# The end of the sink attention: the gate's Silu in three pieces, the last values stored by VectorE, the first two gatings within the stage

## The reference

```python
def attention_mixer(h, norm_w, w_in, q_norm_w, k_norm_w, sinks, w_out):
    u = rms_norm(h, norm_w) @ w_in
    q, k, v, gate = jnp.split(u, [...], axis=-1)
    q = rms_norm(q.reshape(B, L, ATTN_HEADS, ATTN_HEAD_DIM), q_norm_w)
    k = rms_norm(k.reshape(B, L, ATTN_KV_HEADS, ATTN_HEAD_DIM), k_norm_w)
    ...
    o = banded_sink_attention(q, k, v, sinks)
    return (o * jax.nn.silu(gate)) @ w_out
```

## Time and profile before

| | us |
|---|---|
| Median of 3 runs | 1746.34 |
| Lowest, highest run | 1745.02, 1746.79 |
| Profiled execution, device time | 1750.94 |
| Its span in the trace | 1749.1 |
| TensorE busy in the span | 1671.2 |
| VectorE busy | 1188.2 |
| ScalarE busy | 896.5 |

### The profile page before, as it was taken

One profiled execution on the slowest core, in us unless ns is written; L12 is line 12 of the kernel. 1 busy time (PEld: TensorE's weight loads), 2 busy tenths in 40 slices (PEclk: granted clock), 3 DMA queues, 4 the chain that ended last, 5 costly groups with the idle time before them and its releaser, 6 DMA issues. The chain is left out here.

```text
span 1749.1 us, 34014 instructions
## 1 busy us (share of the span) xinstructions
PE 1671.2 (96%) x13060; PEld 1476.5 (84%) x13060; DVE 1188.2 (68%) x2002; ACT 896.5 (51%) x1562; POOL 72.3 (4%) x36
## 2 busy tenths in 40 slices
PE   7989989999999999989999999998989999899989
PEld 7887788899999999988888888896767898788877
DVE  5556566689989799976666666655746656556565
ACT  4335544454554677756666666633545553233333
POOL 0000000100000000000000000000002333100000
PEclk9979989999999999999999999999999999999899
DMA  6532144455555444445666666541123454200004
GB/s 217 181 101 93 49 146 156 158 184 164 180 168 175 137 127 128 133 127 188 193 192 192 192 194 194 174 151 37 61 72 97 145 148 146 81 3 2 3 26 144
DMA packets 63220, 230.06 MB, mean 132 GB/s; under 512 B 7024, under 2 KB 7280, under 8 KB 63104
## 3 DMA queue, kind: packets, MB, share of 16 engines
q1 hardware_dynamic: 63104, 228.44, 41.7%
HBM read 227.36 MB, written 1.05 MB: 131 GB/s over the span
## 5 line engine op out<-in xcount | busy, mean ns | idle before, releaser
L1077 DVE TENSOR_TENSOR tile_low<-weights,tile_high 128x1024 fp32r<-128x1024 f32 x252 | 307.1, 1221 | 143.1 <-ACT tile_high L1067 139.5
L1067 ACT ACTIVATE tile_high<-weights 128x1024 fp32r<-128x1024 f32 x252 | 268.2, 1064 | 136.6 <-issue 136.6
L178 ACT ACTIVATE tile_high<-weights 128x1024 fp32r<-128x1024 f32 x169 | 178.4, 1057 | 250.2 <-issue 76.7
L190 DVE TENSOR_TENSOR tile_low<-weights,tile_high 128x1024 fp32r<-128x1024 f32 x146 | 178.1, 1223 | 170.8 <-ACT tile_high L178 145.4
L1129 PE MATMUL banks<-parts,tile_high 128*128 128x256 f32 x2048 | 270.5, 285 | 0.3 <-PEq L999 0.3
L1431 PE MATMUL banks<-tile_high,parts 128*128 128x512 f32 x1024 | 254.6, 391 | 4.7 <-ACT parts L1396 4.7
L1129 PEld LDWEIGHTS banks<-parts,tile_high 128*128 128x128 f32 x2048 | 254.9, 192 | 0.9 <-issue 0.9
L1431 PEld LDWEIGHTS banks<-tile_high,parts 128*128 128x128 f32 x1024 | 193.2, 189 | 45.1 <-issue 4.9
L230 PE MATMUL banks<-parts,tile_high 128*128 128x272 f32 (+1 forms) x1216 | 171.8, 294 | 4.2 <-PEq L465 3.4
L230 PEld LDWEIGHTS banks<-parts,tile_high 128*128 128x128 f32 x1216 | 158.4, 192 | 19.4 <-issue 16.8
L1134 PE MATMUL banks<-parts,tile_low 128*128 128x256 f32 x1024 | 146.2, 286 | 9.2 <-DVE tile_low L1077 9.2
(11 more groups left out here) (383 smaller groups left out, 2265.7 us busy)
## 6 DMA issues: line engine op xcount, KB each, us to landing
weights<-in_peer_u SPq DMA_DIRECT2D x128, 512.0 KB, 3.5
weights<-in_peer_v SPq DMA_DIRECT2D x128, 512.0 KB, 3.5
weights<-in_dn_in SPq DMA_DIRECT2D x49, 512.0 KB, 3.5
weights<-in_in_t SPq DMA_DIRECT2D x19, 512.0 KB, 3.6
weights<-in_attn_t SPq DMA_DIRECT2D x19, 512.0 KB, 3.6
weights<-in_in_m SPq DMA_DIRECT2D x16, 512.0 KB, 3.6
weights<-in_wq SPq DMA_DIRECT2D x16, 512.0 KB, 3.5
weights<-in_dn_out SPq DMA_DIRECT2D x16, 512.0 KB, 3.5
```

Source lines behind the costliest of these rows:

```text
L178: k.nc.scalar.activation(k.high[:, m % 2, :], k.ring.view(n), ACT.Copy).then_inc(*k.high_made.up())
L190: unit.tensor_tensor(k.low[:, m % 2, :], k.ring.view(n), k.high[:, m % 2, :].bitcast(F32), ALU.subtract).then_inc(*k.low_made[engine].up())
L1067: k.nc.scalar.activation(k.high[:, (s + j) % 2, :], k.ring.buf[:, j % RING, :], ACT.Copy).then_inc(k.high_made.sem, 1)
L1077: k.nc.vector.tensor_tensor(k.low[:, (s + j) % 2, :], k.ring.buf[:, j % RING, :], k.high[:, (s + j) % 2, :].bitcast(F32), ALU.subtract).th ...
```

## The change

The Silu over the gate, one instruction over eight tiles, becomes three: over tiles 0 and 1 straight behind the last gate copy, and so ahead of the store of unit 14 and the copies of unit 15; over tiles 2 and 3, and over tiles 4 to 7, behind those copies. ScalarE's loop loses its last iteration. VectorE gets three instructions at the end of its list: the products of value chunks 0 and 1 with their gate, of chunks 2 and 3 with theirs, each after the Silu piece of the same number and after a count of stores, and the copy of unit 15's values out of PSUM, which ScalarE made before. `out_rows` is told by `opened=2` that two of the four gatings are done: it leaves them out on VectorE, ScalarE doesn't wait for them, and the counts of the other two move down by two.

```diff
@@ -1508,6 +1508,9 @@
     dve.wait_ge(*sig.last())
 
 
+OPENED = 2
+
+
 def sink_attention_stage(k):
 
 
@@ -1517,6 +1520,7 @@
     scaled, turned, unturned, summed = k.start("att_scaled", "att_turned", "att_copied", "att_valued")
     stored, stats, gated = k.start("att_stored", "att_stats", "gate_made")
     fills = AH // 2
+    silu, opened = k.start("gate_silu", "gate_opened")
     gate_tile = lambda i: k.tiles["attn_g"] + i
     ahead = dict(zip(range(2, 18, 2), [gate_tile(i) for i in range(AHEAD, fills)] + list(early(k, "attn_out"))))
     high, low = k.pair(L)
@@ -1634,6 +1638,15 @@
                     scale(u - 1)
                 if u in ahead:
                     make_low(dve, k, ahead[u])
+            for c in range(OPENED):
+                dve.wait_ge(*silu.at(c + 1))
+                dve.wait_ge(*stored.at(len(units) - 4 + 2 * c))
+                pair = k.y2[:, 2 * c:2 * c + 2, :]
+                nc.vector.tensor_tensor(pair, pair, T[:, GATE + 2 * c:GATE + 2 * c + 2, :], ALU.mult).then_inc(*opened.up())
+            tt, a = units[-1]
+            dve.wait_ge(*summed.at(len(units)))
+            nc.vector.tensor_copy(k.y2[:, a, META + tt * P:META + tt * P + P],
+                                  ps[:, value_bank(len(units) - 1), 0:P]).then_inc(*opened.up())
 
         @block.scalar
         def _(act):
@@ -1666,7 +1679,7 @@
                 nc.scalar.activation(k.y2[:, a, cols], ps[:, value_bank(u), 0:P], ACT.Copy).then_inc(*stored.up())
 
             stats2, = k.start("att_meta_copied")
-            for u in range(len(units) + 2):
+            for u in range(len(units) + 1):
                 if u < len(units):
                     exps(u)
                 if u in ahead:
@@ -1674,14 +1687,16 @@
                 if u and u % 2 == 0:
                     act.wait_ge(k.ring.used.sem, gate_tile(u // 2 - 1) + 1)
                     nc.scalar.activation(T[:, GATE + u // 2 - 1, :], fill, ACT.Copy).then_inc(*gated.up())
-                if u >= 2:
+                if u == len(units):
+                    act.wait_ge(*gated.at(fills))
+                    nc.scalar.activation(T[:, GATE:GATE + 2, :], T[:, GATE:GATE + 2, :], ACT.Silu).then_inc(*silu.up())
+                if 2 <= u <= len(units):
                     store(u - 2)
                 if 1 <= u <= len(units):
                     copy_turned(u - 1)
-                if u == len(units):
-                    act.wait_ge(*gated.at(fills))
-                    nc.scalar.activation(T[:, GATE:GATE + fills, :], T[:, GATE:GATE + fills, :],
-                                         ACT.Silu).then_inc(*gated.up())
+            for c, n in ((2, 2), (4, fills - 4)):
+                nc.scalar.activation(T[:, GATE + c:GATE + c + n, :], T[:, GATE + c:GATE + c + n, :],
+                                     ACT.Silu).then_inc(*silu.up())
 
 
 def heads_stage(k, xs, weights, spans):
@@ -1831,7 +1846,7 @@
     if stop <= 24: return
     out_rows(k, "attn_out", [(k.hm, 0, META, 0)] + [(k.h[:, tt, :], 2 + 2 * tt, P, META + tt * P) for tt in range(NT)],
              k.y2, k.tiles["dn_in"] + RING, k.T2[:, 10:18, :],
-             following="dn_in", scale=[None] + [k.norms[:, 24 + 3 + tt:24 + 4 + tt] for tt in range(NT)])
+             following="dn_in", opened=OPENED, scale=[None] + [k.norms[:, 24 + 3 + tt:24 + 4 + tt] for tt in range(NT)])
     if stop <= 25: return
     deltanet(k, tiles, stop)
 
@@ -2841,7 +2856,7 @@
     peer(k, stop)
 
 
-def out_rows(k, name, tiles, x, prefetch, gate=None, send=None, scale=None, following=None):
+def out_rows(k, name, tiles, x, prefetch, gate=None, send=None, scale=None, following=None, opened=0):
 
 
     nc, ps, first = k.nc, k.ps, k.tiles[name]
@@ -2869,8 +2884,8 @@
             for q in range(pairs):
                 if q >= 4:
                     act.wait_ge(k.ring.used.sem, first + 2 * (q - 4) + 2)
-                if gate is not None:
-                    act.wait_ge(*gated.at(q + 1))
+                if gate is not None and q >= opened:
+                    act.wait_ge(*gated.at(q - opened + 1))
                 nc.scalar.activation(high_x[:, place(q), :], x[:, 2 * q:2 * q + 2, :], ACT.Copy).then_inc(*x_high.up())
                 for half in range(2):
                     make_high(act, k, first + 2 * q + half)
@@ -2887,7 +2902,7 @@
         @block.vector
         def _(dve):
             def open_gate(q):
-                if gate is not None and q < pairs:
+                if gate is not None and opened <= q < pairs:
                     pair = x[:, 2 * q:2 * q + 2, :]
                     nc.vector.tensor_tensor(pair, pair, gate[:, 2 * q:2 * q + 2, :], ALU.mult).then_inc(*gated.up())
```

## The result

The changed kernel takes **1750.28 us** (median of 12 runs, 1748.73 to 1751.7) against 1746.34 us before (12 runs, 1745.02 to 1751.34): a ratio of 1.002, 95% interval 1.0013 to 1.0028. It is slower by about 3.9 us, or 0.2%. The forecast was 1743.8 us.

The account below looks back on a forecast made before the run. TensorE, busy 96% of the span, was taken as the bound, with its idle times and low clock. An earlier start (1.77 us) plus clock (0.74) gave 2.5 us off 1746.34: 1743.8 us, range 1741.6 to 1746.0.

Parts of the forecast that it names:

- What fills the idle time, and the chain.: Two TensorE idle times before the output projection; moving Silu, gatings and last store starts the projection 1.77 us earlier.
- delay of the last values: First Silu and table load ahead of ScalarE's last copies make TensorE start the last values 0.19 us later.
- VectorE's copy: After the last values, VectorE copies them out of PSUM in 0.27 us, no longer behind the Silu.
- change of stage: From the attention stage's last instruction to ScalarE's first cast of the output projection: 0.29 us.
- cast to first matmul: At the output projection's start, from ScalarE's first cast to TensorE's first matmul: 0.80 us.
- The table load costs its 1.28 us and no drain; one load for three pieces.: On ScalarE, Silu's load adds no 1.38 us drain, and Silu pieces after Copies need no new load.
- The clock at the start: At the projection's start the granted clock stays low 3.4 us, losing 1.52 us instead of 2.26: 0.74 gained.
- Whatever the start of that stage gains is passed on to the end of the kernel: Behind the projection's start nothing waits for a late DMA or engine, so the start's 1.77 us reaches the end.
- Rival (4): Slower: clock falls at the projection's restart and stays low far longer; 0.5 to 3.6 us slower; chance 0.05.
- It would make the clock's part of this gain vary from execution to execution.: At the projection's start, the clock monitor's free-running window would make the clock's share, forecast at 0.74 us, vary.
- The profile as a sample of the kernel before: Profiled execution, 1750.94 us, stood 4.6 us above the median; the same gain was taken from the median 1746.34.

Follow-up runs that it names:

- e5: Kernel before, with useless matmuls filling three kinds of TensorE breaks in the delta stage; 1743.17 us, ratio to before 0.9976.
- e6: Changed kernel, with useless matmuls filling three kinds of TensorE breaks in the delta stage; 1739.82 us, ratio to before 0.9955.
- e3: Changed kernel with four more useless matmul calls (2.7 us) at the end of its output projection; 1746.48 us, ratio to before 0.9996.
- e4: Kernel before with the 2.7 us of useless matmuls at the end of the output projection; 1757.31 us, ratio 1.0051.
- e12: Changed kernel with delta-stage breaks filled, plus useless calls ahead of the last values and at the output projection's head; 1739.58 us, ratio to before 0.9962.
- e1: Kernel before, run again without edit; 1748.12 us (10 runs), ratio 0.9997.
- e9: Kernel before, run once more without edit for another trace; 1746.65 us (one execution).
- e7: Changed kernel with the first two gatings back at the head of the output projection; 1745.96 us, ratio to before 0.9992.
- e2: Changed kernel, run again without edit; 1750.74 us, ratio to before 1.0014.
- e10: Changed kernel with the last values stored by ScalarE behind the third Silu piece, not by VectorE; 1746.38 us, ratio to before 0.9998.

## Why the prediction was wrong

- **What fills the idle time, and the chain.** Right. Each term: delay of the last values 0.19 forecast, 0.11 measured; VectorE's copy 0.27, 0.29; change of stage 0.29, 0.29; cast to first matmul 0.80, 0.80; in all 1.77 forecast, 1.83 measured.
- **The table load costs its 1.28 us and no drain; one load for three pieces.** Right; 1.30 us from its start to that of Silu.
- **The clock at the start: low for 3.4 us, 0.74 us back.** Right: low for 3.4 us, 0.70 us back.
- **"Whatever the start of that stage gains is passed on to the end of the kernel".** Wrong, and this is the step that failed. It put what the clock does behind the projection at nothing: the 2.58 us of lead at the head of the delta stage met 6.16 us of longer windows there (3.4 us more of low clock in the first window, 3.4 in the third, 10.2 in the fourth, 3.4 less in the fifth). The row that I gave for it ends at 1325 and says nothing of the time behind. I had tested the step against DMAs and other engines, for which it held here. I had seen that the clock falls at one of equal breaks of 2.01 us and not at another, and used that for the place of the change alone. The same rows say that the time behind depends on when each break comes. The later breaks, filled, give the gain back (e5, e6); behind 2.7 us of added work the kernel takes 7 us less (e3) or 7 us more (e4) than a plain sum.
- **Rival (4)** had the right sign and the right price per microsecond of low clock (0.447; 4.70 us for 10.2 is 0.46), at the wrong place: it asked for one long stretch at the restart, and found the dense matmuls there an argument against it. The low stretches came in the delta stage, whose small matmuls are what surrounds them in rows 9 and 10.
- **"It would make the clock's part of this gain vary from execution to execution."** At the start of the projection it did not: the low stretch there is 6.8 us in all profiles with one Silu, and 3.4 us in all with three pieces, but for e12, which has none. The first fall comes between 88.3 and 90.5 us in these profiles (101.2 in e12), but by the sink stage the fall comes 7.27 to 7.44 us after the last but one values in all thirteen profiles where it falls there at all. So the kernel has come into step with the clock by then. This holds less well in the delta stage: the kernel before comes to it at 235.87 us in e1 and 235.82 in e9, and has the costly stretch in one and not in the other. What brings it into step was not tried.
- **The profile as a sample of the kernel before.** It stood 4.6 us above its median. I carried the gain over to the median as it was, without asking where that gap came from. Against e9 it is 3.1 us of low clock in the delta stage and 1.2 us ahead of the change. The long stretch stood in rows 10; I read it as a price at another place, and not as something that other executions lack and that a shift can move.

What stays open: which shift gives which falls. The table has no order that a rule could be read from, and nothing between its rows was tried.

## What to carry to other kernels

Where a trace has several short breaks of TensorE among small matmuls, with the granted clock low behind some of them, a gain ahead of them is not passed on as it is: list the breaks behind the change, and put their low stretches into the range on both sides (here the change, e3, e4 and e7 came out 5.6 to 7.3 us off the plain sum, for edits of 0.8 to 2.7 us). Fill those breaks first, with useless matmuls that fit into the wait, and judge other edits after that: the fills were worth 3.9 and 10.9 us here, more than the 2.58 us of the edit, and only behind them did the edit show its own worth. Before trusting one profile as the baseline, look at a second one when its time is far from the median.

## What the runs showed of the hardware

- 2.7 us of added work made one kernel 4.3 us faster (e3 against e2) and the other 10 us slower (e4), by low stretches of TensorE's granted clock of 3.4, 6.8 and 10.2 us. In the delta stage 10.2 us of low clock cost 4.7 us, and 3.4 us cost 1.5 to 1.6.
- At breaks of 2.01 us between small matmuls the clock fell or did not fall, at the same instruction. Timeline of the changed kernel; the clock fell 0.17 us before the end of the first break, and 1.01 us after the end of the second, where e9 and e3 have no fall at either:

```profile
1605.37 3.53 PE L2210 MATMUL banks<-big 64*64 64x128 f32 x32 [2.01 <-DVE big L2412]
...
1645.15 2.77 PE L2210 MATMUL banks<-big 64*64 64x128 f32 x32 [2.00 <-DVE big L2412]
```

- Of two subtractions on VectorE and GpSimd that began within 0.23 us of each other the later one took longer: 3.23 us instead of 1.22 on VectorE (e10), 3.44 instead of 2.39 on GpSimd (the changed kernel).
